# Two transformer blocks on one core: the compressed softmax in halves by four heads, turned copies ahead of pass ends, the entrance strip emptied in three parts

## The reference

```python
# first block (cut)
o_a = dsa_attention(q_a, k_a, v_a, q_i, k_i, w_i)     # 8 heads of 64, causal, top-128 keys by an index
o_b = causal_attention(q_b, k_b, v_b)                 # 8 heads of 96 (queries, keys), values of 64
p_m = softmax(einsum('bqhd,bmhd->bhqm', q_m, k_m) * M_HEAD_DIM ** -0.5)   # 4 heads of 128, 256 memory rows
ys  = stack([o_a * silu(z_a), o_b * silu(z_b), o_m * silu(z_m)])
x   = x + einsum('bsnd,nbsd->bsd', sigmoid(gate_logits), einsum('nbsw,nwd->nbsd', ys, w_branch)) @ w_out
# second block, attention of one group (cut)
s_c = einsum('bqghd,bngd->bghqn', qb, k_cmp) * scale
p_c = masked_softmax(s_c, cmp_end <= t)               # 31 compressed keys
o_c = einsum('bghqn,bngd->bqghd', p_c, v_cmp)
o   = gb[..., 0:1] * o_c + gb[..., 1:2] * o_s + gb[..., 2:3] * o_w
```

## Time and profile before

| | us |
|---|---|
| median of 3 runs | 1437.97 |
| lowest, highest | 1437.46, 1438.49 |
| the profiled execution | 1438.1 |
| its span, first to last instruction | 1436.2 |

### The profile page before, as it was taken

How to read it: one execution, slowest core, us unless ns; L and a number is a source line. 1 busy time by engine, 2 the same in 40 slices (tenths; PEclk the granted TensorE clock), 3 DMA queues, 4 the chain that set the end, 5 groups by cost and what they waited for, 6 DMA issues and landing times.

```text
span 1436.2 us, 21003 instructions
## 1 busy us (share of the span) xinstructions
PE 1412.9 (98%) x7707; PEld 1185.6 (83%) x7707; DVE 873.9 (61%) x1650; ACT 667.3 (46%) x1177; POOL 612.7 (43%) x433
## 2 busy tenths in 40 slices
PE   9999999999999999999999999999999999999998
PEld 7888789778778888889997777788888888888886
DVE  4345986565763262843566677772264878777776
ACT  5354555567573333343434567773225433323342
POOL 5433654444353444154443356663416332333330
PEclk9999999999999999999999999999999999999999
DMA  6323433203102675869672210004265433333221
GB/s 215 91 74 88 144 98 93 62 12 94 45 1 73 206 251 192 278 203 313 238 235 66 67 31 1 2 1 158 92 231 174 152 103 103 104 105 110 90 88 59
DMA packets 89114, 170.30 MB, mean 119 GB/s; under 512 B 7031, under 2 KB 22978, under 8 KB 89026
## 3 DMA queue, kind: packets, MB, share of 16 engines
q1 hardware_dynamic: 79298, 140.72, 31.1%
q10 hardware_dynamic: 9728, 28.39, 5.5%
HBM read 148.12 MB, written 20.97 MB: 118 GB/s over the span
## 4 chain that ended last, share of the span: by engine, by line
PE 90%; DVE 4%; ACT 2%; issue 1%; DMA 1%; POOL 1%; SPq 0%; POOLq 0%; DVEq 0%; ACTq 0%
PE bank L1042 58%; PE bank L1735 9%; PE bank L1312 4%; PE bank L1320 4%; PE bank L1134 3%; PE bank L1104 3%; PE bank L965 3%; PE bank L1002 1%; PE bank L1136 1%; DMA raw<-in_w_in 1%; PE bank L1723 1%; PE bank L1554 0%; DVE xt_lo L2989 0%; DMA raw<-in_w_out 0%; DVE proj L2977 0%
## 5 line engine op out<-in xcount | busy, mean ns | idle before, releaser
L802 POOL TENSOR_TENSOR w_lo<-raw,w_hi 128x1024 fp32r<-128x1024 f32 (+3 forms) x185 | 435.5, 2365 | 494.1 <-ACT w_hi L1811 494.1
L1811 ACT ACTIVATE w_hi<-raw 128x1024 fp32r<-128x1024 f32 (+3 forms) x189 | 191.1, 1015 | 376.7 <-DMA raw<-in_w_in 176.6
L1042 PE MATMUL bank<-xt_hi,w_hi 128*128 128x512 f32 x560 | 221.4, 395 | 1.3 <-ACT proj L1908 1.3
L1042 PE MATMUL bank<-xt_hi,w_lo 128*128 128x512 f32 x560 | 218.4, 390 | 0.0
L1042 PE MATMUL bank<-xt_lo,w_hi 128*128 128x512 f32 x560 | 218.1, 389 | 0.0
L1042 PE MATMUL bank<-w_hi,xt_hi 128*128 128x512 f32 (+2 forms) x520 | 191.4, 368 | 0.0
L1042 PE MATMUL bank<-w_lo,xt_hi 128*128 128x512 f32 (+2 forms) x520 | 189.3, 364 | 0.0
L1042 PE MATMUL bank<-w_hi,xt_lo 128*128 128x512 f32 (+2 forms) x520 | 189.3, 364 | 0.0
L1042 PEld LDWEIGHTS bank<-xt_hi,w_hi 128*128 128x128 f32 x560 | 105.2, 188 | 24.6 <-issue 2.2
L1042 PEld LDWEIGHTS bank<-xt_hi,w_lo 128*128 128x128 f32 x560 | 105.2, 188 | 22.1
L1042 PEld LDWEIGHTS bank<-xt_lo,w_hi 128*128 128x128 f32 x560 | 105.3, 188 | 21.6 <-issue 0.5
(11 more groups left out here) (457 smaller groups left out, 2948.6 us busy)
## 6 DMA issues: line engine op xcount, KB each, us to landing
raw<-in_w_in SPq DMA_DIRECT2D x72, 512.0 KB, 3.5
raw<-in_w_ff SPq DMA_DIRECT2D x36, 512.0 KB, 3.7
quarter_b<-in_w_ff SPq DMA_DIRECT2D x28, 512.0 KB, 3.5
raw<-in_w_in SPq DMA_DIRECT2D x24, 392.0 KB, 4.4
w_hi<-sums_hi SPq DMA_DIRECT2D x16, 512.0 KB, 5.4
w_lo<-sums_lo SPq DMA_DIRECT2D x16, 512.0 KB, 6.5
raw<-in_w_branch SPq DMA_DIRECT2D x12, 512.0 KB, 3.8
chunk_a<-in_w_out ACTq DMA_DIRECT2D x12, 512.0 KB, 4.8
```

The costliest lines, as they stand in the source:

```text
L802: pool.tensor_tensor(w_lo[:, slot, 0:halves, 0:width], raw[:, slot, 0:halves, 0:width], w_hi[:, slot, 0:halves, 0:width].bitcast(F32), ALU ...
L1042: ins = pe.matmul(o, lhs, rhs, start=st and j == 0, stop=en and j == 2)
L1811: act.activation(w_hi[:, slot, 0:halves, 0:width], raw[:, slot, 0:halves, 0:width], ACT.Copy)\
```

## The change

**The compressed softmax goes by quads.** Maximum, subtraction, exponential, sum and scaling, each one instruction on 1024 elements (the sum step three), become two on 512 elements, four heads each. The table gives a pair number for each of the four (group 0 quad 0 and 1, group 1 quad 0 and 1). In the first group the exponentials move from pair 2 to pair 1, the sums from pair 5 to pairs 2 and 9, the scalings from 6 to 4 and 11, the transposes from 8 and 9 to 7 and 15. In the second group the maxima move from 24 to 25 and 31, the subtractions from 27 to 27 and 35, the exponentials from 27 to 29 and 37 (and behind the position's own exponentials), the sums from 30 to 33 and 41, the scalings from 32 to 35 and 43, the transposes from 40 and 41 to 39 and 47. Quad 1 is now transposed into the other output bank and no longer waits for ACT's copy of quad 0.

**Copies in front of pass ends.** `empty` moves from the end of one position to the next, behind its `copy_turned`.

**Entrance strip.** In `"a"` and `"n"` tile 0 is emptied at position 4 and tile 1 at position 5. In `"b"` tiles 0 and 1 stay at position 3, in front of `copy_turned`. PE waits for tile 1 only where bank 5 is written.

**Kept rows first.** In `"b"` ACT's four copies of the first branch's rows (`ys_a[0]`, L2123, pairs 20 to 23) stand in front of the pair's exponentials instead of behind. In "rows" DVE's inverse sums stand between the two parts of `take_compressed`.

The diff, cut to its core:

```diff
-CMP_MAX, CMP_SHIFT, CMP_EXP, CMP_SUM, CMP_NORM, CMP_T = (1, 24), (1, 27), (2, 27), (5, 30), (6, 32), (8, 40)
+CMP_MAX, CMP_SHIFT, CMP_EXP = (1, 1, 25, 31), (1, 1, 27, 35), (1, 1, 29, 37)
+CMP_SUM, CMP_NORM, CMP_T = (2, 9, 33, 41), (4, 11, 35, 43), (7, 15, 39, 47)
...
-                    if stage == "n" and u - u0 in (2 * CMP_NORM[0], 2 * CMP_NORM[1]):
-                        g = CMP_NORM.index((u - u0) // 2)
-                        pool.wait_ge(sem["cmp_rsum"], g + 1)
-                        pool.tensor_tensor(sc_c, sc_c, csum[:].unsqueeze(3).to_broadcast([P, TT, HEADS, 32]), ALU.mult)\
+                    if stage == "n" and (u - u0) % 2 == 0 and (u - u0) // 2 in CMP_NORM:
+                        n = CMP_NORM.index((u - u0) // 2)
+                        z = of_quad(n)
+                        pool.wait_ge(sem["cmp_rsum"], n + 1)
+                        pool.tensor_tensor(sc_c[:, :, z], sc_c[:, :, z],
+                                           csum[:, :, z].unsqueeze(3).to_broadcast([P, TT, HEADS // 2, 32]), ALU.mult)\
...
-                if quad == 0:
-                    pe.wait_ge(sem["cmp_normed"], g + 1)
-                    pe.wait_ge(sem["o_emptied"], first_pass)
-                else:
-                    pe.wait_ge(sem["cmp_copied_a"], g + 1)
+                pe.wait_ge(sem["cmp_normed"], 2 * g + quad + 1)
+                if g == 0 and quad == 0:
+                    strip_scaled(STRIP_M2 + 3)
+                pe.wait_ge(sem["o_emptied"], first_pass + quad)
                 for i in range(TT):
-                    ins = pe.transpose(bank[4 + (first_pass + 1) % 2][:, i * P:(i + 1) * P],
+                    ins = pe.transpose(bank[4 + (first_pass + 1 - quad) % 2][:, i * P:(i + 1) * P],
                                        proj[:, i, KC2 + P * quad:KC2 + P * quad + P], ident)
                 ins.then_inc(sem["cmp_t"], 1)
...
-                pe.wait_ge(sem["cmp_copied_a"], g + 1)
-                pe.wait_ge(sem["cmp_copied_d"], g + 1)
+                pe.wait_ge(sem["cmp_copied_d" if quad else "cmp_copied_a"], g + 1)
...
-            ENTRY = {"a": (STRIP_GATE0, 1), "b": (STRIP_GATE1, 2), "n": (STRIP_M2 + 3, 3)}
+            ENTRY = {"a": (STRIP_GATE0, 1), "b": (STRIP_GATE1, 3), "n": (STRIP_M2 + 3, 4)}
...
-                    strip_scaled(entry_strip_)
+                    pe.wait_ge(sem["gate_half"], half_no + 1)
...
+                    if w["first"] and w["pas"] == STAGE_PASSES[stage][0] + 1 and stage != "b":
+                        strip_scaled(entry_strip_)
...
+                    if stage == "b" and is_step(e) and e - p0 in (20, 21, 22, 23):
+                        t = e - p0 - 20
+                        if t == 0:
+                            act.wait_ge(sem["o_emptied"], STAGE_PASSES["a"][1] + HEADS // 2)
+                        act.activation(ys_a[0][:, t, :], proj[:, t, YTA:YTA + S], ACT.Copy).then_inc(sem["ysa_hi"], 1)
...
-                    if nsa and is_step(e) and e - p0 in CMP_EXP:
-                        act.wait_ge(sem["cmp_shifted"], CMP_EXP.index(e - p0) + 1)
-                        act.activation(sc_c, sc_c, ACT.Exp).then_inc(sem["cmp_exp"], 1)
-                    if nsa and is_step(e) and e - p0 in CMP_T:
-                        g = CMP_T.index(e - p0)
...
+                    for n in range(4):
+                        if nsa and e - p0 == CMP_EXP[n]:
+                            v = sc_c[:, :, of_quad(n)]
+                            act.wait_ge(sem["cmp_shifted"], n + 1)
+                            act.activation(v, v, ACT.Exp).then_inc(sem["cmp_exp"], 1)
...
-                LAG_EMPTY = LAG_T + 2
+                LAG_EMPTY = LAG_T + 3
...
+                        if stage == "b":
+                            empty_entrance(stage, (0, 1))
                     copy_turned(entry(stage, pos - LAG_T))
+                    emptied_pair = entry(stage, pos - LAG_EMPTY)
+                    if is_step(emptied_pair) and UNITS[2 * emptied_pair + 1]["last"]:
+                        empty(UNITS[2 * emptied_pair + 1]["pas"])
                     if pos == AHEAD - 1:
-                        empty_entrance(stage, 0)
-                    if pos == AHEAD + (stage != "b"):
-                        empty_entrance(stage, 1)
+                        empty_entrance(stage, (2, 3))
+                    if stage != "b" and pos in (AHEAD + 1, AHEAD + 2):
+                        empty_entrance(stage, (pos - AHEAD - 1,))
                     if e in KEY_TURNS:
                         keep_keys(e, score_banks(stage, pos)[1])
                     if e == "rows":
-                        take_compressed(1, score_banks(stage, pos))
+                        take_compressed(1, 0, score_banks(stage, pos))
+                        sums_inverse(entry(stage, pos - 1))
+                        take_compressed(1, 1, score_banks(stage, pos))
                     if is_step(e):
                         mask_step(stage, pos)
-                    if pos != AHEAD:
...
+                        for n in range(4):
+                            if e - p0 == CMP_MAX[n]:
+                                largest_compressed(n)
+                        for n in range(4):
+                            if e - p0 == CMP_SHIFT[n]:
+                                shift_compressed(n)
+                            if e - p0 == CMP_SUM[n]:
+                                sum_compressed(n)
...
-                    p = entry(stage, pos - LAG_EMPTY)
-                    if is_step(p) and UNITS[2 * p + 1]["last"]:
-                        empty(UNITS[2 * p + 1]["pas"])
...
+            def sum_compressed(n):
+
+                z, c = of_quad(n), csum[:, :, of_quad(n)]
+                dve.wait_ge(sem["cmp_exp"], n + 1)
+                step(dve.tensor_reduce(c, sc_c[:, :, z], AX.X, ALU.add))
+                step(dve.reciprocal(c, c))
+                dve.tensor_tensor(c, c, gsig[:, :, 12 * n:12 * n + 12:3], ALU.mult).then_inc(sem["cmp_rsum"], 1)
```

82 lines of the change are left out of this document (37 added, 45 removed).

## The result

| | before | after |
|---|---|---|
| median of 6 runs, us | 1437.73 | 1430.75 |
| lowest, highest | 1437.14, 1438.49 | 1430.13, 1430.88 |
| the profiled execution, its span | 1438.1, 1436.2 | 1430.88, 1429.0 |

The account below looks back on a forecast made before the run. PE was taken to bound the kernel, idle 8.7 us in the three attention stages. Gains 0.8 + 0.5 + 5.4 less 1.9 of new waits made 4.8 us, so 1433.2 us by the median; range 1430.8 to 1436.2.

Parts of the forecast that it names:

- Stage a, 0.8: Stage a: gain of 0.8 us, from two pass ends at 0.26 each plus 0.3 at the entrance.
- Stage b, 0.5: Stage b: entrance 0 (bounds -0.2 and +0.4), and 0.5 us at its end from the earlier rows' copy (bounds 0.3 and 0.6).
- Stage n, what comes, 1.9: Stage n: new waits from the halves, 0.6 exponentials, 0.7 subtractions, 0.3 sum step, 0.3 scaling; 1.9 us, bounds 0 and 5.
- The exponential at 37: Stage n, pair 37: exponential half of 0.55 us ahead of ACT's copy, cover 0.25, so 0.3 us lost.
- the sum step at 33: Stage n, pair 33: half of 1.15 us puts the next masks some 0.6 later; with cover 0.25, 0.3 us lost.
- the scaling at 35: Stage n, pair 35: half of 1.0 us ahead of a short pair, POOL made late by the subtraction; 0.3 us lost.
- The single row taken for the cover: Stage n: ACT's copy ends at 859.04, PE comes at 859.29; this 0.25 us was the cover for exponentials and sum step.
- the forecast's own rule: Stage n: a half step takes half the whole step's time plus 0.07 us for a fixed part.
- Stage n, what goes, 5.4: Stage n: waits removed, 1.6 + 1.2 + 1.0 + 0.5 + 0.6 + 0.3 + 0.2 = 5.4 us.
- Entrance and rows in n, 0.5: Stage n: the 0.3 us wait for `prob_t` at the entrance goes, and 0.2 from the earlier inverse sums in "rows".
- All halves are covered: Rival, stage n: idle time of the engines covers every half, so gain 6.7 us, 1431.3; chance 0.17.
- POOL's chain: Rival: mask, exponential, inverse, scaling binds at most of the removed waits, so gain only 2.0 us, 1436.0; chance 0.17.

## Why the forecast was wrong, point by point

The sign, the stages and the waits that go were right. The gain was 2.2 us too small, and nearly all of that lies in stage n, where two steps failed. The term for what comes was put at 1.9 us and measured 0.8. And the waits that go were priced by their listed idle time, 4.9 us for the softmax, where PE lost 5.9 by its rows; the sum had no term for that.

- **Stage a, 0.8: 0.97.** The pass ends gave 0.47 of the 0.52, the entrance 0.50 instead of 0.3.
- **Stage b, 0.5: 0.21.** Two errors that nearly cancel, which is luck. The entrance was put at 0 and gave 0.26, inside its bounds: PE's wait there is now 0.24 us for the copy (at 377.20) instead of 0.40 for the tiles. The last pairs were put at 0.5 and gave -0.05. The rows' copies are worth 0.51, but the swap of the pass ends takes 0.57 (48.63 to 48.06 when undone). The step that failed is that the swap got no term in b. The only reason on record for a free swap, "the masks behind both start when they did", was worked out for stage a, at a place where the copy had no wait; in b it has one.
- **Stage n, what comes, 1.9: 0.8.** The exponential at 29 costs 0.38 (forecast 0.3) and the subtraction at 35 costs 0.4 (forecast 0.6). The exponential at 37 costs 0, since the compressed transposes of pair 39 stand in PE's list between the copy and its reader; I had used "products come ahead of the transposes" for other halves and overlooked it for this one. No wait is put down to the sum step at 33 or the scaling at 35 (forecast 0.3 each); no run takes them out alone. The subtraction at 27 shows no wait either, but the eight transposes behind it (887.59) last 1.21 us and those at 883.52 1.03, so up to 0.2 may be missing in the 0.8. The single row taken for the cover, 0.25 us at 859.04, doesn't stand for all positions. By the forecast's own rule the exponential half is 0.60 us and not 0.55; it takes 0.62, and the sum step's half the 1.15 that were assumed.
- **Stage n, what goes, 5.4.** The softmax alone gained 5.30 net with some 0.8 of new costs, so 6.1 went where its terms said 4.9. The listed idle time that went in that kernel is 4.8 us (0.93 + 0.46 + 0.21 + 1.20 + 0.70 + 0.57 + 0.75). The other part was inside PE's busy time, here from n's first scores to a us behind its last, before and with the softmax alone, each with 1237 instructions:

```profile
822.02:964.44 142.42, 136.30 (x1237) 113.20 (x1237) 106.81 (x400) 101.58 (x320) 87.01 (x129) 1.00 0.03 9
```

```profile
822.61:959.73 137.12, 135.43 (x1237) 113.34 (x1237) 106.95 (x410) 101.31 (x322) 87.12 (x131) 1.00 0.04 10
```

That is 0.87 us less busy time. Most of it is how a wait is listed. Two places in the kernel before, one with a wait and one without:

```profile
839.73 0.28 PE L1136 MATMUL bank<-k_parts,q_parts 128*128 128x256 f32 x1
840.94 0.88 PE L1312 MATMUL bank<-cst,sc 128*128 128x128 f32 x6 [0.93 <-DVE proj L2801]
...
859.17 0.28 PE L1136 MATMUL bank<-k_parts,q_parts 128*128 128x256 f32 x1
859.29 0.82 PE L1312 MATMUL bank<-cst,sc 128*128 128x128 f32 x6
```

Without a wait the transposes start 0.12 us after the last product, whose row of 0.28 us runs on beside them. In front of a wait all 0.28 us count as busy. From start to start it is 1.21 us against 0.12, so the wait costs 1.09 us where 0.93 are listed. Counted so, the seven waits that the softmax took away (at 840.94, 845.03, 846.38, 893.00, 899.45, 905.96 and 919.00) were 5.9 us instead of 4.8, and its two new ones are 0.7 instead of 0.4: together 0.7 of the 0.87 us. Under 0.2 us net are left for transposes that last longer because their second unit is late (1.31 us for eight at 905.96 in the kernel before, 1.04 at 850.76). That loss the prediction had named at its start ("plus what transposes lose inside their own run") and given half a us in the range; the larger one it had not seen.

- **Entrance and rows in n, 0.5: 0.6.** Only together with the rest; alone 0.28.
- **The rivals.** "All halves are covered" was nearest in time (1431.3), but not in its mechanism: two halves cost 0.8, and what the waits had cost beyond their listed time gave more than that. POOL's chain took over nowhere. A cost of the fixed part of more DVE instructions was named from the Trainium skill, VectorE: DVE Perf Modes (section "The TRN2 errata"), 0.7 us of DVE work as an estimate for 12 instructions. There are 10 more (1650 to 1660), and DVE's busy time went from 873.9 to 874.1 us over the whole span, so this trace doesn't show the 0.7.
- **What would show it.** Idle time under 0.4 in a: yes. About 1 in b: 1.14. 2 to 3.5 in n: 1.29, below. The wait for the copy in b: at 377.20, which is 378.2 on the clock of the kernel before. New waits after pairs 29 and 33 to 35: 0.22 and 0.23. After 37: none. The first two of these on PE's timeline of the changed kernel:

```profile
377.20 0.44 PE L1320 MATMUL bank<-cst,allow 128*128 128x128 f32 x2 [0.24 <-DVE prob_t L2811]
...
891.80 0.85 PE L1320 MATMUL bank<-cst,sc 128*128 128x128 f32 x6 [0.22 <-issue]
```

Left open: what the second output bank is worth by itself, what the halves at 27, 33 and the scaling at 35 cost inside PE's busy time, and why the swap of the pass ends costs 0.56 us in n beside the old softmax and 0.11 beside the new one.

## What to carry to other kernels

Before two instructions of an engine are swapped, look whether the one that goes first has to wait at that place: work that stood in front of it ran in that wait, and behind it it is on the path. Cutting a step helped here only where each piece met idle time of its engine between itself and the next instruction that somebody waits for; distance in the order is not cover, and two halves of the sum step placed back to back held their engine for longer than the whole. Moving the whole steps to better places had gained more (2.9 us) than cutting them there (2.4). Compare kernels by the length of a stage between two rows that both have, and price a wait from start to start of the rows around it: the listed idle time was 0.07 to 0.17 us short at each of the seven waits that went.

## What the runs showed of the hardware

- One idle time of PE of 2.06 us, in a stretch where it is otherwise busy, was followed by two us at a granted clock of 0.50 and two at 0.73. The idle times of 0.93 and 1.20 us in the kernel before and one of 1.28 us in the kernel with the entrance alone left it at 1.00. The cost behind the wait was nearly as large as the wait.
- Two halves take 8 to 17% more busy time than a whole: sums, maxima and subtractions 0.67 us each against 1.20, exponentials 0.62 against 1.06, scalings 1.04 against 1.92. The small instructions of the sum step shrink least: the inverse of 16 numbers takes 0.25 us, that of 32 took 0.35.
- A subtraction of DVE with both inputs in SBUF (512 elements, 0.67 us) costs POOL about 0.4 us, whichever scaling it meets; the one of 1024 elements cost 0.9 (2.42 against 1.53 us).
- A row of PE's timeline runs past the start of the next one: products of 256 columns last 0.28 us and start 0.12 us apart. So PE's busy time holds 0.16 us more in front of a wait than without one.
